# Layer 0's convolution input computed from rounded parts, step by step, instead of in plain float32

## The reference, cut to what matters

```
mod = silu(c) @ w_ada[l] + b_ada[l]              # six rows of 1024; shift sh1 and scale sc1 are the first two
h   = rmsnorm(x, n1) * (1 + sc1) + sh1           # 384 x 1024
a_q, ..., z, xbc, dt_raw = split(h @ w_in)       # xbc: 768 columns, dt_raw: 16
xbc = silu(conv(xbc)); dt = softplus(dt_raw + dt_bias)
```

## Time and profile before

| | |
|---|---|
| median of 3 runs | 782.83 us (782.64 to 782.89) |
| the profiled execution, its own time | 782.79 us |
| its span (first to last instruction) | 780.9 us |
| PE busy | 738.8 us, 95% |
| DVE / ACT busy | 583.1 us, 75% / 502.8 us, 64% |
| chain that ended last | PE 74%, DVE 11%, ACT 9% |
| HBM read | 182.79 MB, 237 GB/s over the span |

### The profile page before, as it was taken

How to read it: one execution, slowest core, us unless ns; L and a number is a source line. 1 busy time by engine, 2 the same in 40 slices (tenths; PEclk the granted TensorE clock), 3 DMA queues, 4 the chain that set the end, 5 groups by cost and what they waited for, 6 DMA issues and landing times.

```text
span 780.9 us, 10972 instructions
## 1 busy us (share of the span) xinstructions
PE 738.8 (95%) x4019; PEld 573.5 (73%) x4020; DVE 583.1 (75%) x968; ACT 502.8 (64%) x834; POOL 50.4 (6%) x36
## 2 busy tenths in 40 slices
PE   4999999899999999999999999989999999999994
PEld 2557877457966888888769788845698788888874
DVE  4258386986666899999858746879666789999965
ACT  3048693574457777777646678457456887777852
POOL 0001352000000000000000135200000000000000
PEclk9999999999999999999999999999999999999998
DMA  9963034977338899999864113096831189999902
GB/s 365 423 244 109 14 121 168 423 271 272 109 116 366 316 369 366 379 368 350 327 240 153 58 52 103 33 382 211 303 128 55 55 327 379 375 363 376 370 18 84
DMA packets 33489, 186.26 MB, mean 239 GB/s; under 512 B 5136, under 2 KB 6288, under 8 KB 16400
## 3 DMA queue, kind: packets, MB, share of 16 engines
q1 hardware_dynamic: 33424, 185.42, 62.9%
HBM read 182.79 MB, written 2.62 MB: 237 GB/s over the span
## 4 chain that ended last, share of the span: by engine, by line
PE 74%; DVE 11%; ACT 9%; issue 4%; DMA 1%; ACTq 0%; DVEq 0%; SPq 0%
PE psum L875 22%; PE psum L1022 11%; PE psum L904 11%; PE psum L1224 5%; PE psum L989 4%; PE psum L705 3%; PE psum L927 3%; PE psum L853 2%; DVE att L2260 1%; ACT split L1415 1%; PE psum L741 1%; PE psum L1092 1%; PE psum L756 1%; PE psum L888 1%; PE psum L1106 1%
## 5 line engine op out<-in xcount | busy, mean ns | idle before, releaser
L2049 DVE TENSOR_TENSOR split<-ring,split 128x2048 fp32r<-128x2048 f32 x96 | 219.9, 2291 | 26.8 <-ACT split L1540 25.3
L1540 ACT CAST split<-ring 128x2048 fp32r<-128x2048 f32 x96 | 183.6, 1913 | 21.9 <-PE psum L904 14.5
L875 PE MATMUL psum<-split,y_hi 128*128 128x512 f32 x512 | 160.8, 395 | 0.4 <-ACT selT L1513 0.4
L875 PEld LDWEIGHTS psum<-split,y_hi 128*128 128x128 f32 x512 | 93.7, 188 | 18.6 <-issue 0.5
L875 PE MATMUL psum<-split,y_lo 128*128 128x512 f32 x256 | 100.1, 391 | 0.0
L1022 PE MATMUL psum<-ring_r,hT_hi 128*128 128x512 f32 x216 | 73.2, 393 | 0.0
L904 PE MATMUL psum<-split,hidT 128*128 128x512 f32 x256 | 69.7, 394 | 1.8 <-DVE hidT_lo L2054 1.8
L904 PEld LDWEIGHTS psum<-split,hidT 128*128 128x128 f32 x256 | 47.3, 188 | 14.2 <-DVE hidT_lo L2054 4.8
L875 PEld LDWEIGHTS psum<-split,y_lo 128*128 128x128 f32 x256 | 48.1, 188 | 10.2
L2490 POOL TENSOR_TENSOR ud<-const,da_hi 128x1024 fp32r<-128x1024 f32 x12 | 27.3, 2293 | 397.8 <-DVE da_lo L2150 390.3
L1022 PEld LDWEIGHTS psum<-ring_r,hT_hi 128*128 128x128 f32 x216 | 40.0, 188 | 9.0 <-issue 0.7
(11 more groups left out here) (314 smaller groups left out, 1425.6 us busy)
## 6 DMA issues: line engine op xcount, KB each, us to landing
ring<-in_w_gu SPq DMA_DIRECT2D x64, 1024.0 KB, 5.8
ring<-in_w_ada SPq DMA_DIRECT2D x40, 1024.0 KB, 6.6
ring<-in_w_down SPq DMA_DIRECT2D x32, 1024.0 KB, 5.7
ring<-in_w_rows SPq DMA_DIRECT2D x12, 1024.0 KB, 5.1
ring<-in_first SPq DMA_DIRECT2D x8, 1024.0 KB, 14.7
ring<-in_w_out SPq DMA_DIRECT2D x8, 1024.0 KB, 5.8
ring<-in_w_xbc SPq DMA_DIRECT2D x8, 800.0 KB, 9.1
par<-in_par SPq DMA_DIRECT2D x1, 1728.0 KB, 14.1
```

Source lines behind the costliest of these rows:

```text
L875: last = pe.matmul(dst, x[:, g, t, :], w[:, j, :], start=(t == 0 and i == 0), stop=(t == KD - 1 and i == 2))
L1540: act.copy(splits[unit_split(n)][:, 0, :], slot(key)).then_inc(raised("whi", l, p), 1)
L2049: tt(lo, slot(unit_key(l, p, n)), hi.bitcast(F32), ALU.subtract).then_inc(raised("wlo", l, p), 1)
```

## The change

```diff
-ROUNDED = (1,)
+ROUNDED = (0, 1)
...
+        if key in (("xbc", 0, 0), ("xbc", 0, 1)):
+            last_use[b] = pieces.index(("first", 0, 5)) + 0.1 * (key[2] + 1)
...
 # ScalarE
                         if not (l or arg[0]):
                             act.wait_ge(setup_dve, 1)
+                            x_split(0, 0)
...
                                 act.copy(ada_rows[:, 0:2 * P], bank(key)[:, 0:2 * P]).then_inc(*was_read(key))
-                                if j == KD - 2:
-                                    for p in range(2):
-                                        split_win(0, p)
+                                if j in (1, 3, 5):
+                                    x_split(0, 1 + j // 2)
+                                act.wait_ge(*modulated(0, 0, j))
+                                act.copy(hT_hi[:, j, :], h_f[:, j, :]).then_inc(sig["hx_hi"], 1)
+                                if j >= KD - 2:
+                                    split_win(0, j - (KD - 2))
...
 # VectorE, norm(l, n)
+                if not l:
+                    x_rest_split(0, 0)
...
+                def moved(c):
+                    for j, part in ((0, slice(0, P)), (1, slice(P, TOK))):
+                        ins = ts(h_f[:, c, part], hT[:, c, part], amul[:, l, n, c, j:j + 1], mods[:, l, SH1 + c, j:j + 1],
+                                 ALU.mult, ALU.add)
+                    return ins
+                def rest_of(c):
+                    dve.wait_ge(*hx("hx_hi", l, c))
+                    tt(hT_lo[:, c, :], h_f[:, c, :], hT_hi[:, c, :].bitcast(F32), ALU.subtract).then_inc(sig["hx_lo"], 1)
+                if not l:
+                    groups = {0: (0, 1), 1: (1, 2), 2: (2, 4), 4: (4, KD)}
+                    scaled(0, 1).then_inc(dve_step, 1)
+                    dve.wait_ge(dve_step, dve_steps())
+                    for c in range(KD):
+                        first(c)
+                        moved(c).then_inc(sig["h"], 1)
+                        if c + 1 in groups:
+                            scaled(*groups[c + 1]).then_inc(dve_step, 1)
+                            dve.wait_ge(dve_step, dve_steps())
+                        dve.wait_ge(*modulated(0, 0, c))
+                        rest_of(c)
+                        if c in (1, 3, 5):
+                            x_rest_split(0, 1 + c // 2)
+                        if c == 4:
+                            tables()
+                        if c >= KD - 2:
+                            split_win(0, c - (KD - 2))
+                    return
```

More of the change, by code:

```diff
@@ L294, in build @@
                     pieces.append(("first", 0, 0))
-                for i in range(2 if l in ROUNDED else 0, KD // 2):
+                for i in range(2 if l else 0, KD // 2):
                     pieces.append(("xbc", l, i))
@@ L301, in build @@
             elif s[0] == "ada":
-                if s[2:] == (1, 0) and l in ROUNDED:
+                if s[2:] == (1, 0) and l:
                     pieces += [("xbc", l, 0), ("xbc", l, 1)]
@@ L321, in build @@
     for l in ROUNDED:
-        held_by.update({("win", l, 0): ("ada", l, 1, 0), ("win", l, 1): ("ada", l, 1, 1),
-                        ("win", l, 2): ("xbc", l, 0), ("win", l, 3): ("xbc", l, 1)})
+        if l:
+            held_by.update({("win", l, 0): ("ada", l, 1, 0), ("win", l, 1): ("ada", l, 1, 1),
+                            ("win", l, 2): ("xbc", l, 0), ("win", l, 3): ("xbc", l, 1)})
         del held_by["h_hi", l, 0], held_by["h_hi", l, 1]
@@ L348, in build @@
             b = H_AT + 1 - key[2]
-        elif key in [("ada", x, 1, k) for x in ROUNDED for k in (2, 3)]:
+        elif key in [("ada", 1, 1, k) for k in (2, 3)]:
             b = H_AT + 3 - key[3]
@@ L357, in build @@
         last_use[b], last_key[b] = n, key
-    more_slots = [b for b in range(HELD, RING) if b not in [place["xbc", l, i] for l in ROUNDED for i in range(2)]]
+        if key in (("xbc", 0, 0), ("xbc", 0, 1)):
+            last_use[b] = pieces.index(("first", 0, 5)) + 0.1 * (key[2] + 1)
+    more_slots = [b for b in range(HELD, RING) if b not in [place["xbc", l, i] for l in ROUNDED if l for i in range(2)]]
     for l in range(DEPTH):
@@ L539, in build @@
                 ("dt_r", 1), ("da", 1), ("bss", 3), ("brs", 3), ("prep", 3), ("ud", 3), ("ud_lo", 3), ("da_lo", 1), ("xd", 3), ("yx", 3),
-                ("mhi", 4), ("mlo", 4), ("mixhi", 4), ("ohi", 1), ("olo", 1), ("wb", 3), ("dtd", 1), ("skip", 3), ("seg", 6), ("in_hi", PARTS + 2), ("in_lo", PARTS + 3), ("zs", 1), ("nb", PAIRS), ("es", PAIRS // 2), ("pn", PAIRS), ("yz", 1), ("yrs", 1), ("yn", 1),
+                ("mhi", 4), ("mlo", 4), ("mixhi", 4), ("ohi", 1), ("olo", 1), ("wb", 3), ("dtd", 1), ("skip", 3), ("seg", 6), ("in_hi", PARTS), ("in_lo", PARTS), ("zs", 1), ("nb", PAIRS), ("es", PAIRS // 2), ("pn", PAIRS), ("yz", 1), ("yrs", 1), ("yn", 1),
                 ("flag", 1), ("top", 2), ("shares", 2), ("chosen", 2), ("hhi", 6),
@@ L634, in spent @@
             return done[key][0], 1
-        IN_FRONT = (("w0", "w1", "h0", "h1"), ("w0", "w1"))
+        IN_FRONT = (("w0", "w1"), ("w0", "w1"))
         IN_HI = [{name: n + 1 for n, name in enumerate(front + ("w2", "w3", "w4", "w5"))} for front in IN_FRONT]
         IN_LO = [{name: n + 1 for n, name in enumerate(front + middle + ("w3", "w4", "w5"))}
-                 for front, middle in zip(IN_FRONT, (("h2", "w2"), ("w2",)))]
+                 for front, middle in zip(IN_FRONT, (("w2",), ("w2",)))]
         def in_hi(l, name):
@@ L1429, in x_split @@
                 if i == 2:
-                    act.wait_ge(sig["wx_spent"], ROUNDED.index(l) + 1)
+                    act.wait_ge(sig["wx_spent"], per["wx_spent"] * ROUNDED.index(l) + 1)
                 elif i == 3:
@@ L1488, in norm @@
                     act.activation(src[:, 0:TOK], src[:, 0:TOK], ACT.Exp, scale=-0.5).then_inc(sig["rstd"], 1)
-                if l not in ROUNDED:
+                if l != 1:
                     return
@@ L1590, in _ @@
                             split_win(l, arg[0])
-                        if l in ROUNDED and arg[0] == 0:
+                        if l and arg[0] == 0:
                             x_split(l, 3)
@@ L1878, in parts_of @@
                     dve.wait_ge(sig["hx"], per["hx"] * (l - 1) + (1, 2, 3, 3, 4, 4, 4, 4)[c])
+                    moved(c).then_inc(dve_step, 1)
+                    dve.wait_ge(dve_step, dve_steps())
+                    rest_of(c)
+                def moved(c):
                     for j, part in ((0, slice(0, P)), (1, slice(P, TOK))):
@@ L1881, in parts_of @@
                                  ALU.mult, ALU.add)
-                    ins.then_inc(dve_step, 1)
-                    dve.wait_ge(dve_step, dve_steps())
+                    return ins
+                def rest_of(c):
                     dve.wait_ge(*hx("hx_hi", l, c))
                     tt(hT_lo[:, c, :], h_f[:, c, :], hT_hi[:, c, :].bitcast(F32), ALU.subtract).then_inc(sig["hx_lo"], 1)
+                if not l:
[7 more added lines that the diff above has]
+                            scaled(*groups[c + 1]).then_inc(dve_step, 1)
+                            dve.wait_ge(dve_step, dve_steps())
+                        dve.wait_ge(*modulated(0, 0, c))
+                        rest_of(c)
+                        if c in (1, 3, 5):
[5 more added lines that the diff above has]
+                    return
                 if l in ROUNDED:
@@ L1901, in norm @@
                     return
[L1902 to L1920, removed]
             def tables():
```

## The result

The changed kernel takes 795.64 us (median of 4 runs, 793.41 to 797.98) against 782.75 (782.64 to 782.89): 1.0156 times the kernel before, with an interval of 1.014 to 1.0172, slower by 12.9 us. Forecast was 789.4, with a range up to 792.0. The sign held, and in the head of layer 0 the mechanism; the size did not, and a third of the loss arises behind the head, where the forecast had put nothing.

What follows compares the result with a forecast made beforehand. PE was taken to bound layer 0's head. Steps -4.8 us, start and lo(1) +1.1, chunks 4 to 7 +0.2, `par` +5.8, clock +1.6, step 7 +1.2, `dt_rows` +1.6: about +6.6 on 782.8, giving 789.4 (784.4 to 792.0).

Steps and rivals of the forecast that it cites:

- Steps: PE's steps in layer 0's head: 4.9 us each instead of 5.51, eight of them saving 4.8 us.
- lo(1): End of `hT_lo` for chunk 1 on DVE: at 23.4 us, after step 0 ends at 22.6, so step 1 starts late.
- lo(3): End of `hT_lo` for chunk 3 on DVE: at 33.4 us, after step 2 ends at 33.2.
- `par`: Step 4: table load issued at 39.2 us behind f7, landed 47.8; DVE waits for it, PE stands 5.8 us before `first(6)`.
- Steps 6 and 7: PE stalls late in layer 0's head: 1.2 us ahead of step 7 and 1.6 us for `dt_rows`.
- The clock, the first mis-sized term: Slow products on PE behind the 5.8 us gap in step 4: 1.6 us, bounds 0 and 2.0.
- The head in all: Layer 0's head, up to the start of `rows`: 68.2 us instead of 61.6, 6.6 us later.
- the delay is carried whole to the end: Everything behind 61.6 us hangs on PE and its slots, so the head's 6.6 us delay reaches the end unchanged.
- the clock stays up: Rival: PE's clock does not fall in the 5.8 us gap; 787.8 us, chance 0.18.
- The splits at 6 and 7 remain: Rival: waiting for `par` costs nothing, late-step splits do; `rows` at 63.2, 784.4 us; chance 0.14 for small or no wait.
- All covered: Rival: splits and `par` hide in ACT's and DVE's idle time; `rows` at 57.7, 778.9 us, chance 0.08.
- `par` still later: Rival: w0 and w1 share the queue, so `par` lands up to 2 x 2.5 us later; up to 794.4 us, chance 0.08.

Runs made afterwards that it cites:

- b: Changed kernel with par as late as it was, but tables() moved behind chunk 7 on DVE; 1.0104 times the kernel before, 791.1 us.
- a: Changed kernel with par issued before x3 instead of behind f7; 1.0033 times the kernel before, 786.55 us against 783.37.
- c: As a, with the lower part of w0 moved behind chunk 7 and that of w1 behind side_taps(1) on DVE; 1.0007 times the kernel before.
- d: Changed kernel with 26 unread float32 products of ones on PE ahead of first(6); 1.0079 times the kernel before, 790.28 us.
- h: As c, with 16 tiny products, then 18 float32 products of ones, on PE ahead of the first norm's sums; 0.9979 times the kernel before.
- after_again: The changed kernel measured once more, unaltered, beside the kernel before; 1.0158 times, 796.31 us against 783.85.
- i: Kernel before with 49 tiny products (98 records) on PE ahead of the first norm; one run, 790.43 us against 783.79.
- f: Kernel before with 60 tiny products (120 records) on PE ahead of the first norm; 1.0021 times the kernel before, 785.65 us.
- j: As c, with 16 tiny products (32 records) on PE ahead of the first norm; one run, 784.39 us.
- g: As c, with 52 tiny products (104 records) on PE ahead of the first norm; 0.9981 times the kernel before, 782.2 us against 783.85.

## Why the prediction missed

Its own steps, in order:

- **Steps.** 4.9 us forecast, 4.82 measured; the cost of 0.2 us for a float32 block between rounded products was about right. lo(1) and lo(3) came last in their steps, as forecast. Step 0 began at 18.7 instead of 17.75; half of that is the later start of the sums. x0 could be rounded from 12.40, right at the limit that the forecast had named.
- **`par`.** Issue forecast 39.2, measured 39.91; landing 47.8 and 48.7. Queue order held: `par` took 8.8 us behind f7, and w0 behind it held up ACT in b. The gap on PE: 5.8 forecast, 6.2 measured. a and b show that this wait is the largest part.
- **Steps 6 and 7.** Stalls of 1.2 and 1.6 forecast, 0.9 and 1.4 measured; c removes nearly all of both by moving two instructions of DVE.
- **The clock, the first mis-sized term.** 1.6 us forecast, 2.3 measured in the gap's wake (after against d). The bounds, 0 and 2.0, came from the norm's six records at the start; the slow stretch behind the gap lasted until 55 to 56 us, longer than those six records.
- **The head in all.** It is 8.7 us behind instead of 6.6. PE comes back at 49.5 where the forecast had 48.2: 0.9 of this is the later landing of `par`, 0.4 what DVE and PE take behind it (0.8 where 0.4 was reckoned); in the 0.9 is a start of the sums 0.5 later, which is not the change's (the profiles of both heads begin them anywhere from 9.6 to 10.2, h at 10.8). The slow clock adds 0.7, the two stalls are 0.5 shorter, and the stretch from `dt_rows` to `rows` takes 2.9 instead of 2.3, in part since the clock falls again at its end.
- **The step that failed: "the delay is carried whole to the end".** The forecast treated all behind 61.6 us as rigid, and so put nothing there. Carried it was, although not all of it hangs on PE (the chain of before runs through ACT and DVE from 96.6 to 109.8 us): from 88 to 248 us after stays 9.7 to 9.9 behind. But more came on top, 4.3 us up to the last norm: 1.2 in `rows`, where the clock fell a second time at 69.3 (17.54 for 16.37 us, and back to 16.35 when the gap is gone in a); 1.4 at the start of the experts, of which the chain shows 10.04 for 8.41 us of the same 36 products at half clock; and 2.0 from there to layer 1's ada products, with the 1.6 of the stall; 0.3 came back. The first is in both profiles of the changed kernel and so goes with it, but not by way of the stalls at 62.5 and 66 alone: a has the same two, 1.44 and 1.39 us, at a clock of 1.00. The second comes and goes: after_again has none there and another at 532. The third hangs on the place in PE's program: i brings it into the kernel before, and in f and j it stands in the last norm instead. So the last two are accidents of this build and this execution; no working of the head could have given them.
- **The rival "the clock stays up"** is excluded: PEclk is 0.50 behind the gap in after, and d shows what that costs. **"The splits at 6 and 7 remain"** was a fair picture of a: `rows` at 63.2 and 784.4 forecast for no wait at all, `rows` at 62.7 and 1.0033 x 782.8 = 785.4 measured, with 1.6 us of it the stall. **"All covered"** needed `par` before 42; even then it isn't reached unless the rests of w0 and w1 move as well: `rows` at 59.3 in c and 58.4 in g, 57.7 forecast.
- **"`par` still later"** by sharing the queue with w0 and w1: the trace speaks against it, 8.8 us from issue to landing for `par`, 8.6 forecast.

What stays open: why the clock falls at 69.3 with PE busy and stalls of only 0.9 and 1.4 us behind it, while the same two stalls leave it at 1.00 in a; and what PE waits for in the norms.

## What to carry to other kernels

Before a piece of a ring is held longer or a slot is given up, follow every transfer that the issuing engine sends behind the pieces affected, the tables among them: here two slots fewer moved a table by 11.6 us, and one line that issues it earlier gave back 9.6 of 12.9 us. A short wait in an in-order queue is to be placed behind everything that another engine needs soon: `tables()` for PE's bank, the rests of w0 and w1 for the next modulation. And a long stall on PE is to be priced higher than its length: here 2.3 us of slow clock behind 6.2 us, and 1.2 more in a second drop that followed; two stalls of 1.4 us without such a gap ahead of them cost only their length (a).

## What the runs showed of the hardware that was not expected

- Two kernels that differ only in idle records on PE ahead of the first norm differ in time elsewhere: 98 records more in the kernel before gave a stall of 2.81 us in layer 1's norm, 120 more gave one of 2.07 us in the last norm; in c_rests_late 0 more gave 1.28 us in layer 1's norm, 32 more 2.64 us in the last one, 104 more none.
- Products put ahead of a slow stretch to bring the clock up moved the slow stretch behind the next idle time (h: 1.45 instead of 2.75 us for the sums, then 1.94 instead of 1.07 for a block of `first`).
- The changed kernel's runs spread over 4.6 us (793.41 to 797.98) where the kernel before's spread over 0.25 beside it (elsewhere over up to 3.4, 782.22 to 785.62); of its two profiles one lost the clock at 264, the other at 532 us.
